# Expert weights of a MoE layer in longer DMA runs, with the columns reordered in the conversions

## The reference

```python
def swiglu(x, w_gu, w_dn):
    g, u = jnp.split(x @ w_gu, 2, axis=-1)
    return (jax.nn.silu(g) * u) @ w_dn

def moe_swiglu(x, router, w_gu, w_dn):
    logits = jnp.einsum('btd,de->bte', x, router).astype(jnp.float32)
    top_v, top_i = lax.top_k(logits, TOP_K)              # 2 of 8
    top_w = jax.nn.softmax(top_v, axis=-1)
    ...
    for e in range(N_EXPERTS):
        out = out + comb[..., e:e + 1] * swiglu(x, w_gu[e], w_dn[e])
    return out
```

## Time and profile before

| | |
|---|---|
| median of 3 runs | 1185.72 us (1184.89 to 1187.89) |
| the profiled execution | 1185.72 us, span 1184.0 us |
| mean granted clock of TensorE | 0.986 |
| busy over the span | PE 95%, DVE 80%, ACT 61% |
| MoE stage | about 745 to 1134 us of the span |
| DMA rate | mean 245 GB/s, in the MoE stage 390 to 394 in most slices |

### The profile page before, as it was taken

How to read it: one execution, slowest core, us unless ns; L and a number is a source line. 1 busy time by engine, 2 the same in 40 slices (tenths; PEclk the granted TensorE clock), 3 DMA queues, 4 the chain that set the end, 5 groups by cost and what they waited for, 6 DMA issues and landing times.

```text
span 1184.0 us, 31432 instructions
## 1 busy us (share of the span) xinstructions
PE 1126.7 (95%) x13839; PEld 996.1 (84%) x13839; DVE 948.7 (80%) x1011; ACT 721.0 (61%) x716; POOL 24.9 (2%) x59
## 2 busy tenths in 40 slices
PE   7999999999999999899999998899989998989997
PEld 4888888878888888688888885788989988988976
DVE  5986896786666657996788678499899899899877
ACT  4555744446555445445574436687888787688653
POOL 4000001000000001000000100000000000000000
PEclk7999999999999999999999999899999999999999
DMA  9665566645656563456565665699999999999911
GB/s 268 219 211 182 178 213 196 200 143 183 202 184 210 182 212 125 142 167 213 191 205 190 205 201 195 233 367 390 394 392 393 392 393 393 380 393 393 366 50 37
DMA packets 195672, 289.55 MB, mean 245 GB/s; under 512 B 5208, under 2 KB 132200, under 8 KB 195543
## 3 DMA queue, kind: packets, MB, share of 16 engines
q1 hardware_dynamic: 193830, 283.71, 68.8%
q0 software_dynamic: 1728, 4.16, 1.3%
HBM read 286.53 MB, written 1.52 MB: 243 GB/s over the span
## 4 chain that ended last, share of the span: by engine, by line
PE 78%; DVE 16%; ACT 3%; issue 2%; DMA 0%; SPq 0%; DVEq 0%; ACTq 0%
PE acc L600 16%; PE acc L602 16%; PE acc L601 16%; DVE wl L1367 10%; PE acc L879 4%; PE acc L881 3%; PE acc L882 3%; PE acc L914 2%; PE acc L585 2%; PE acc L592 2%; PE acc L586 2%; PE acc L931 2%; PE acc L934 2%; PE acc L933 2%; PE aux L832 2%
## 5 line engine op out<-in xcount | busy, mean ns | idle before, releaser
L1367 DVE SCALAR_TENSOR_TENSOR wl<-raw,wh 128x2048 f16<-128x2048 f32 x179 | 408.6, 2287 | 116.1 <-ACT wh L1012 115.4
L600 PE MATMUL acc<-xn,wh 128*128 128x264 f16 x1424 | 393.0, 276 | 0.6 <-DVE wl L1367 0.6
L602 PE MATMUL acc<-xn,wl 128*128 128x264 f16 x1424 | 393.0, 276 | 0.0
L601 PE MATMUL acc<-xn,wh 128*128 128x264 f16 x1424 | 393.0, 276 | 0.0
L1012 ACT ACTIVATE wh<-raw 128x2048 f16<-128x2048 f32 x179 | 340.2, 1907 | 7.7 <-PE acc L934 3.2
L879 PE MATMUL acc<-ga,wh 128*128 128x96 f16 x1536 | 204.3, 207 | 8.2 <-issue 4.7
L881 PE MATMUL acc<-ga,wh 128*128 128x96 f16 x1536 | 204.0, 207 | 3.9 <-issue 3.8
L882 PE MATMUL acc<-ga,wl 128*128 128x96 f16 x1536 | 204.0, 207 | 3.7 <-issue 3.7
L879 PEld LDWEIGHTS acc<-ga,wh 128*128 128x128 f16 x1536 | 151.3, 98 | 12.1 <-issue 11.5
L600 PEld LDWEIGHTS acc<-xn,wh 128*128 128x128 f16 x1424 | 139.3, 98 | 21.9 <-ACT wh L1012 0.8
L601 PEld LDWEIGHTS acc<-xn,wh 128*128 128x128 f16 x1424 | 139.3, 98 | 21.0
(11 more groups left out here) (304 smaller groups left out, 1861.7 us busy)
## 6 DMA issues: line engine op xcount, KB each, us to landing
raw<-in_w_in SPq DMA_DIRECT2D x56, 1024.0 KB, 5.1
raw<-in_moe_w_gu SPq DMA_DIRECT2D x38, 1024.0 KB, 13.0
raw<-in_ffn_w_gu SPq DMA_DIRECT2D x24, 1024.0 KB, 5.2
raw<-in_moe_w_dn SPq DMA_DIRECT2D x22, 1024.0 KB, 15.1
raw<-in_ffn_w_dn SPq DMA_DIRECT2D x12, 1024.0 KB, 5.1
ya<-in_moe_w_gu SPq DMA_DIRECT2D x11, 1024.0 KB, 14.1
xn<-in_moe_w_gu SPq DMA_DIRECT2D x11, 1024.0 KB, 13.8
xb<-in_moe_w_gu SPq DMA_DIRECT2D x10, 1024.0 KB, 14.4
```

Source lines behind the costliest of these rows:

```text
L600: nc.tensor.matmul(bank, hi, x[:, 0, x0 + k, :], start=(k == 0), stop=False)
L601: nc.tensor.matmul(bank, hi, x[:, 1, x0 + k, :], start=False, stop=False)
L602: last = nc.tensor.matmul(bank, lo, x[:, 0, x0 + k, :], start=False, stop=(k == k_chunks - 1))
L1367: op(V.scalar_tensor_tensor(out=wl[:, s, 0:size], in0=raw_slot[raw_turn(n)[0]][:, 0:size], scalar=WS, in1=wh[:, s, 0:size], op0=ALU.mult, ...
```

## The change

A gate/up unit becomes two chunks of rows by 1024 columns, so that a run has 4 KB; four such units (`BLOCK`) make a block of 1024 columns, and an expert has three blocks: gate columns 0 to 1023; gate 1024 to 1535 with up 0 to 511; up 512 to 1535. A block fills banks 0 and 1 of `acc`. ScalarE evacuates both banks after the fourth unit. A down unit takes, of 512 rows of w_dn, the rows 4p to 4p + 3 for partition p, in two units of two rows: one run of 8 KB in each partition. The order of the hidden columns must then match: output tile j of a group of 512 holds columns j, j + 4, j + 8 and so on. This reordering is done in the two conversions of gate/up units, which read the raw slot with a step of four elements and write `wh` and `wl` contiguously.

```diff
-GU_K, DN_K = C // 2, 2
+GU_K, DN_K = 2, 2
+BLOCK = C // GU_K
...
+def tiles_first(n, raw):
+    return raw.rearrange("p (a j) -> p j a", j=4) if n in GATE_UP else raw
+def like_tiles(n, w):
+    return w.rearrange("p (j a) -> p j a", j=4) if n in GATE_UP else w
...
-            dn = a["moe_w_dn"][0].rearrange("e (c p) m -> p e c m", p=P)
+            dn = a["moe_w_dn"][0].rearrange("e (g p j) m -> p e g (j m)", p=P, j=4)
...
-                            k, col = u % 2 * GU_K, u // 2 % 2 * FE + u // 4 * 512
-                            moe_load(gu_unit(i, u), gu[:, i, k:k + GU_K, col:col + 512], GU_K)
+                            k, col = u % BLOCK * GU_K, u // BLOCK * 1024
+                            moe_load(gu_unit(i, u), gu[:, i, k:k + GU_K, col:col + 1024], GU_K)
                     if i:
-                        moe_load(dn_unit(i - 1, t), dn[:, i - 1, t * DN_K:(t + 1) * DN_K, :], DN_K)
+                        at = t % 2 * UNIT
+                        moe_load(dn_unit(i - 1, t), dn[:, i - 1, t // 2, at:at + UNIT].rearrange("p (k m) -> p k m", k=1), 1)
...
-                nc.scalar.activation(wh[:, s, 0:size], raw_slot[from_slot][:, 0:size], ACT.Copy, scale=WS).then_inc(hi_done, 1)
+                nc.scalar.activation(like_tiles(n, wh[:, s, 0:size]), tiles_first(n, raw_slot[from_slot][:, 0:size]), ACT.Copy,
+                                     scale=WS).then_inc(hi_done, 1)
...
-                op(V.scalar_tensor_tensor(out=wl[:, s, 0:size], in0=raw_slot[raw_turn(n)[0]][:, 0:size], scalar=WS,
-                                          in1=wh[:, s, 0:size], op0=ALU.mult, op1=ALU.subtract), lo_done)
+                op(V.scalar_tensor_tensor(out=like_tiles(n, wl[:, s, 0:size]),
+                                          in0=tiles_first(n, raw_slot[raw_turn(n)[0]][:, 0:size]), scalar=WS,
+                                          in1=like_tiles(n, wh[:, s, 0:size]), op0=ALU.mult, op1=ALU.subtract), lo_done)
```

Around it: the rows of tokens go to banks 2 and 3 of `aux` instead of `acc` (`rows_bank`), so that a down unit waits for the evacuation of the expert before (`down_out`) instead of VectorE's weighting (`ys_ready`), and the gather of the next expert's tokens is split into two halves of two banks, one step apart, with waits for those rows; `gate_or_up` waits for both banks at the start of a block:

```diff
-                elif d == 0 and e:
-                    pe.wait_ge(ys_ready, 2 * e)
+                if d == 0 and e:
+                    pe.wait_ge(down_out, 2 * e)
...
+                    if s == 0 and m % 4 == 0:
+                        if block == 0 and e:
+                            pe.wait_ge(up_out, GROUPS * (e - 1) + m // 4 + 2)
+                        elif block == 1:
+                            pe.wait_ge(gate_out, GROUPS * e + m // 4 + 1)
...
+            nc.scalar.activation(root[:], eps[:], ACT.Silu)
```

More of the change, by code:

```diff
@@ L140, in split_groups @@
     return sum(is_split(i) for i in range(q + 1))
+GATE_UP = {gu_unit(e, u) for e in range(NE) for u in range(MOE_GU)}
+def tiles_first(n, raw):
+    return raw.rearrange("p (a j) -> p j a", j=4) if n in GATE_UP else raw
+def like_tiles(n, w):
+    return w.rearrange("p (j a) -> p j a", j=4) if n in GATE_UP else w
 def ahead(n):
@@ L817, in _, with gather @@
                 pe.nop()
-            def gather(e):
-                for g in range(4):
+            def gather(e, groups):
+                for g in groups:
                     if e:
                         pe.wait_ge(gat_done, 4 * (e - 1) + g + 1)
-                    if e > 3:
+                    if e > 3 and g < 2:
                         pe.wait_ge(sc_done, 8 * (e - 4) + 4 + g + 1)
@@ L827, in gather @@
                         pe.wait_ge(selt_ready, e)
+                    if e > 2 and g > 1:
+                        pe.wait_ge(ys_ready, 2 * (e - 3) + g - 1)
                     for c in (2 * g, 2 * g + 1):
@@ L893, in slots_to_rows @@
                         at = (4 * half + m) * CAP
-                        last = nc.tensor.transpose(acc[0:CAP, ye_bank(e) + half, m * P:(m + 1) * P], yt[:, at:at + CAP],
+                        last = nc.tensor.transpose(rows_bank(e, half)[:, m * P:(m + 1) * P], yt[:, at:at + CAP],
                                                    ident[:])
@@ L939, in _ @@
             pe.wait_ge(sel_ready, 1)
-            gather(0)
+            gather(0, range(4))
             selected_slots(0)
@@ L1244, in _, with gathered @@
                 act.nop()
-            def gathered(e):
-                for g in range(4):
+            def gathered(e, groups):
+                for g in groups:
                     act.wait_ge(gat_full, 4 * e + g + 1)
@@ L1305, in expert_out @@
                     act.wait_ge(ye_full, 2 * e + half + 1)
-                    nc.scalar.activation(ye[0:CAP, 0, half * 512:(half + 1) * 512], acc[0:CAP, ye_bank(e) + half, :],
+                    nc.scalar.activation(ye[0:CAP, 0, half * 512:(half + 1) * 512], rows_bank(e, half),
                                          ACT.Identity, scale=csl[0:CAP, e % 4:e % 4 + 1]).then_inc(ye_hi, 1)
-            gathered(0)
+            gathered(0, range(4))
             selected_slots(0)
@@ L1878, in gate_or_up, with product @@
             def gate_or_up(e, u):
-                n, q = gu_unit(e, u), GROUPS * e + u // 4
+                n, q = gu_unit(e, u), GROUPS * e
                 if n > N_MOE:
                     lo(ahead(n))
-                if u % 4 == 1 and q:
+                if u == 1 and e:
+                    hidden_lo(q - 2)
                     hidden_lo(q - 1)
-                if u % 4 == 3:
-                    b = q % 2
-                    vec_e.wait_ge(gate_out, q + 1)
-                    vec_e.wait_ge(up_out, q + 1)
-                    split = is_split(q)
-                    op(V.scalar_tensor_tensor(out=moe_w[:, b, :] if split else hid_32[:, e % 2, :], in0=moe_g[:, b, :],
+                if u == 9:
+                    hidden_lo(q)
+                def product(g):
+                    b, split = (q + g) % 2, is_split(q + g)
+                    vec_e.wait_ge(gate_out, q + g + 1)
+                    vec_e.wait_ge(up_out, q + g + 1)
+                    vec_e.wait_ge(hid_ready, count[hid_ready])
+                    op(V.scalar_tensor_tensor(out=moe_w[:, b, :] if split else hid_32[:, e % 2, :], in0=moe_g[:, g, :],
                                               scalar=XS if split else XS * WS, in1=moe_u[:, b, :],
                                               op0=ALU.mult, op1=ALU.mult), hid_w)
+                if u == 2 * BLOCK - 1:
+                    product(0)
+                if u == MOE_GU - 1:
+                    product(1)
+                    product(2)
             def down(e, d):
@@ L1903, in expert_out @@
                     vec_e.wait_ge(ye_hi, 2 * e + half + 1)
-                    op(V.scalar_tensor_tensor(out=ye[0:CAP, 1, s], in0=acc[0:CAP, ye_bank(e) + half, :],
+                    op(V.scalar_tensor_tensor(out=ye[0:CAP, 1, s], in0=rows_bank(e, half),
                                               scalar=csl[0:CAP, e % 4:e % 4 + 1], in1=ye[0:CAP, 0, s],
@@ L1917, in _ @@
                             gate_or_up(i, u)
-                            if i > 1 and u == 0:
+                            if i > 1 and u == 1:
                                 expert_out(i - 2)
@@ L1923, in _ @@
                         expert_out(i - 2)
-                    if i + 1 < NE and t == 2:
+                    if i + 1 < NE and t == 3:
                         slot_weights(i + 1)
```

99 lines of the change are left out of this document (58 added, 41 removed).

## The result

The changed kernel takes 1331.31 us (median of 4 runs, 1329.72 to 1333.52); the kernel before, timed beside it, 1186.59 (4 runs). The ratio is 1.1222, with a 95% interval of 1.1205 to 1.1239. The forecast was slower, at 1298 us in a range of 1170 to 1375: sign and mechanism hold, the size was 33 us short (36 in the span of the profiled execution: plus 147.8 us where the working had plus 112).

What follows compares the result with a forecast made beforehand. Transfers, VectorE and TensorE lay within a few per cent, loads held by conversions. VectorE's 477.1 us plus 24 idle makes the stage 501 against 389, plus 112; 1184.0 + 112 = 1296 span, with 1.7 around it 1298 us, range 1170 to 1375.

Steps and rivals of the forecast that it cites:

- Longer runs hidden, worth nothing: MoE loads: transfers 14 to 18 us shorter over eight experts, but no transfer wait left once VectorE is longest.
- The step: Gate/up conversions reading every fourth element: 1.35 us more per conversion on VectorE and ScalarE; likeliest 0.9 to 1.8, chance 0.52.
- The line through the small copies: Step price extrapolated from 64-element copies: about 7 ns more per further 4 bytes, so 21 ns at 16 bytes, 0.33 ns each.
- the doubling for two sources: VectorE's conversion has two sources, so the stall per step was taken as 0.66 ns per element instead of 0.33.
- the upper bound: A whole second step per element in gate/up conversions: 2.14 us more on VectorE, 1.71 on ScalarE.
- VectorE longest by far, 24 us of idle left: MoE stage: VectorE 477.1 us of work against ScalarE 431.5 and TensorE 358.1; 24 of its 41.5 us idle stay.
- Blocks and rows in the auxiliary banks counted as nothing: MoE accumulator handover covered; moved rows worth up to 5 us only where TensorE or ScalarE bounds; both counted as nothing.
- The blocks in expert 0: No down unit between blocks: TensorE waits three times about 1.2 us, put at nothing; 3.6 us without VectorE's backlog as cover.
- The free step: Rival: the conversions' stride costs nothing, so the time falls to 1174 us; chance 0.18.
- The second whole step for each element: Rival: a 16 byte jump doubles the time per element in conversions, 2.14 us on VectorE, 1374 us; chance 0.15.
- The small price: Rival: the conversions' step costs 0.35 to 0.9 us; at 0.6 the time is 1226 us; chance 0.10.
- What would show it: Signs in the MoE stage: VectorE's gate/up conversions near 3.6 us, DMA share near 0.75, VectorE busy over 95%.

Runs made afterwards that it cites:

- e11: Changed kernel with down units of two rows a partition (8 KB runs), 8 byte step in the conversions, row transposes two units later: 1184.57 us.
- e12: Kernel before with only the down units as 8 KB runs and the 8 byte step in the conversions this needs: 1187.03 us, ratio 1.0010.
- e13: Changed kernel with contiguous conversions, the reordering moved to TensorE's weight loads (8 byte steps), row transposes two units later: 1184.46 us.
- e10: Changed kernel with contiguous conversions, down units of 4 KB runs as before, and row transposes two units later: 1183.86 us, ratio 0.9979 to the kernel before.
- e5_old_blocks: Kernel before with the 16 byte step in the conversions and 8 KB down runs, old blocks and banks kept: 1324.48 us, ratio 1.1166.
- e8_first_four: Changed kernel with the first four gate/up units of expert 0 converted without the step: 1321.51 us.
- e1_flat: Changed kernel with both gate/up conversions reading contiguously, everything else kept: 1193.38 us, ratio 1.0061 to the kernel before.
- e9_step32: Changed kernel with gate/up conversions reading in 32 byte steps instead of 16: 1330.79 us.
- e6_act_only: Changed kernel with the 16 byte step on ScalarE's gate/up conversions alone, VectorE's reading neighbours: 1304.32 us.

## Why the prediction was right, and where it was short

*Longer runs hidden, worth nothing.* Right: shown for the 8 KB runs three times over (e11, e12, e13), and for the 4 KB runs only together with the blocks (e10).

*The step.* The step that decided was right in kind and mis-sized. It took 1.35 us for a conversion on both engines; measured are 1.58 on VectorE and 2.00 on ScalarE. VectorE's work in the stage proper grew by 147.1 us instead of 129.6, though that window holds only 92 of the 96 stepped conversions: 17.5 of the 36 us that the span is off. The line through the small copies was the wrong tool: they gave 7 ns on 64 elements for 12 bytes against 8, 0.1 ns an element, while the jump to 16 bytes is 1580 / 2048 = 0.77 ns. That a line through 8 and 12 bytes, doubled, came within 15% of a jump was chance. Whether the doubling for two sources is right stays open: no run here has a VectorE instruction with one source at 16 byte steps. The Trainium skill's table in the Vector Engine (DVE) Microarchitecture Reference (Measured stream behaviour on trn2) gave 1.38 us, an estimate, as close as the line. For ScalarE the upper bound, a whole second step of 1.71 us, was no bound: it took 2.00.

*VectorE longest by far, 24 us of idle left.* Of 41.5 us idle the prediction let 17.5 vanish. In the stage proper 12.7 did, 4.8 less. It is not ScalarE's work that keeps VectorE idle: in e5_old_blocks, with the same step on both engines, the same stretch (first conversion of the stage proper to the last scattered add) has 13.0 us of idle, 18.8 less than before:

```profile
769.04:1275.70 506.66, 378.54 (x7214) 362.28 (x7211) 493.63 (x287) 478.77 (x275) 0.00 (x0) 0.95 0.82 279
```

The 4.8 us thus belong to the rest of the change, the next point. And the start of the stage comes 13.1 us later: 10.6 of it by the four conversions ahead of it, as e8_first_four shows, most of the rest by ScalarE's first conversion of the stage, which VectorE waits for. The prediction had put the four into the sum like any other unit, as if VectorE could do them beside the routing. 17.5 + 4.8 + 13.1 = 35.4 us of the 35.8.

*Blocks and rows in the auxiliary banks counted as nothing.* Wrong by 7 us (e1_flat). The prediction read what the move to `aux` takes away, the 4.1 us, and priced the new waits at the banks of `acc`, but not the one on `sc_done` that the diff adds ahead of the transposes. In the changed kernel it is there too: five pauses, each with ScalarE and then VectorE standing after it, and e5_old_blocks, with the old blocks and banks, is 6.8 us faster. That the banks and not the blocks make this difference is read from where the waits stand; no run moves the transposes alone with the 16 byte step in place. The blocks in expert 0 made TensorE wait 4.2, 6.6 and 4.3 us for evacuations, where the prediction had three times 1.2, but VectorE stood no longer there than in e5_old_blocks (3.2 us against 4.1, from its first conversion of the stage proper to 843 us), so nothing was the right term.

*The rivals.* The free step fell on its condition and on its size: with the step taken away the time was 1193, not 1174, and with the new wait gone as well 1184. Its 92.7 us for a pair of stretches, full on VectorE and full on TensorE in turn, was not reached: e10_rows_late is 2 us faster than before and not 9. What holds it there stays open; its rows show VectorE still waiting 26.4 us for ScalarE's conversions, where it was 31.3. The second whole step for each element is refuted for VectorE, 1.58 of 2.14, and holds on ScalarE, even exceeded. The small price fell on its size, 0.9 us at most. The prediction's own line, a price that grows with the step, is refuted by e9_step32.

*What would show it.* VectorE's conversions near 3.6 us: 3.86, those of the down units still 2.28. VectorE busy over 95%: 494.72 of 513.80 us, 96%. DMA share near 0.75: 0.80. The clock below 1.00, named as a danger: 0.91, though TensorE did not become the bound. One reading was loose: the 8.8 us that ScalarE waited for landings are eight waits, not six; nothing hangs on it. Another left something out: the queue of loads also waited 89.5 us for ScalarE, beside the 139.6 for VectorE.

## What to carry to other kernels

Reorder where the reading instruction has slack: 8 byte steps in f32 were free on VectorE, 16 byte steps cost it 69%, and the reordering moved into the f16 weight loads cost no time. When a tile moves to another buffer, list every wait that the new buffer brings, and find in the trace when its releaser runs in its engine's order, before counting the old wait as a gain. Price the first few units of a stage apart from the rest: work that is hidden in the steady state can stand on the serial path at the start.

## What was not expected of the hardware

ScalarE pays more for a 16 byte step than VectorE, 0.98 ns an element against 0.77, although it has one source, and a little more still when VectorE reads without the step (medians of 3.98 to 4.07 us by slot in e6_act_only, against 3.90 to 3.95). Steps of 16 and 32 bytes cost the same, and the step of 8 bytes costs ScalarE 0.19 us and VectorE nothing. Weight loads with an 8 byte step take 114 ns instead of 98.
